# Mixing stage of a one-core transformer kernel reordered: rotation ahead of splits, gating products last, the two channel halves normalised apart, output projection by consecutive channels

## The reference, cut to what matters

```python
h = rmsnorm_2(x, mix_norm[l])
z = h @ w_in[l]                                   # 1024 x 2560: gate u, gate v, q, k, v, 512 columns each
z_sgu = jax.nn.gelu(z[..., :2 * D_SGU], approximate=False)
q = partial_rotary(q, positions)                  # first 16 of 64 channels of each head
k = partial_rotary(k, positions)
y_a = chunked_spatial_gating(z_sgu, sgu_ln_g[l], sgu_ln_b[l], sgu_w_s[l], sgu_b_s[l])
y_b = dilated_mixture_attention(q, k, v).reshape(b, s, D_ATT)
y = jnp.concatenate([rmsnorm_2(y_a, out_norm_a[l]), rmsnorm_2(y_b, out_norm_b[l])], axis=-1)
x = x + y @ w_out[l]
```

## Time and profile before

| what | value |
|---|---|
| median of three runs | 1241.16 us |
| the profiled execution's own time | 1240.6 us |
| its span, first to last instruction | 1238.6 us |
| mean granted PE clock | 0.992 |
| PE busy | 1199.3 us, 97% |
| DVE busy | 777.5 us, 63% |
| ACT busy | 585.3 us, 47% |
| DMA queue q1, share of 16 engines | 51.5% |
| weights read | 203.04 MB |

### The profile page before, as it was taken

How to read it: one execution, slowest core, us unless ns; L and a number is a source line. 1 busy time by engine, 2 the same in 40 slices (tenths; PEclk the granted TensorE clock), 3 DMA queues, 4 the chain that set the end, 5 groups by cost and what they waited for, 6 DMA issues and landing times.

```text
span 1238.6 us, 17664 instructions
## 1 busy us (share of the span) xinstructions
PE 1199.3 (97%) x7063; PEld 1031.1 (83%) x7063; DVE 777.5 (63%) x838; ACT 585.3 (47%) x724; POOL 63.2 (5%) x81
## 2 busy tenths in 40 slices
PE   6889999999999999999999999999979999999997
PEld 5776888888999988888888888888769988888886
DVE  6955766666654556666667666666573645666665
ACT  5445634343656554444345434345554546434443
POOL 2110000000011200000000000000011000000000
PEclk9999999999999999999999999999998999999999
DMA  8254456565544365656565555565432543556561
GB/s 210 80 141 161 156 181 203 173 199 178 172 161 137 120 187 171 197 176 202 178 195 170 189 184 190 182 198 174 139 102 91 182 137 119 183 191 191 182 203 68
DMA packets 157223, 206.04 MB, mean 166 GB/s; under 512 B 8937, under 2 KB 130353, under 8 KB 157169
## 3 DMA queue, kind: packets, MB, share of 16 engines
q1 hardware_dynamic: 156720, 204.51, 51.5%
q10 hardware_dynamic: 448, 0.77, 0.4%
HBM read 203.04 MB, written 1.05 MB: 165 GB/s over the span
## 4 chain that ended last, share of the span: by engine, by line
PE 88%; DVE 5%; ACT 3%; issue 1%; POOL 1%; DMA 1%; ACTq 1%; SPq 0%; POOLq 0%; DVEq 0%
PE outp L745 26%; PE acc L685 19%; PE outp L685 18%; PE outp L747 13%; PE acc L795 2%; PE outp L703 1%; PE outp L715 1%; PE outp L1156 1%; DVE w_lo L2096 1%; DMA raw<-in_even_w_in_dram 1%; ACT w_hi L1569 1%; ACTq L1784 1%; PE acc L1237 1%; ACT arena L1890 1%; PE acc L1379 0%
## 5 line engine op out<-in xcount | busy, mean ns | idle before, releaser
L1569 ACT ACTIVATE w_hi<-raw 128x2048 fp32r<-128x2048 f32 x177 | 339.5, 1918 | 432.4 <-PE outp L747 291.1
L2096 DVE TENSOR_TENSOR w_lo<-raw,w_hi 128x2048 fp32r<-128x2048 f32 x177 | 405.3, 2290 | 199.0 <-ACT w_hi L1569 199.0
L745 PE MATMUL outp<-h_pair,w_hi 128*128 128x512 f32 x1056 | 374.7, 399 | 0.0
L747 PE MATMUL outp<-h_pair,w_lo 128*128 128x256 f32 x1056 | 296.6, 281 | 0.0
L745 PEld LDWEIGHTS outp<-h_pair,w_hi 128*128 128x128 f32 x1056 | 198.5, 188 | 49.5
L747 PEld LDWEIGHTS outp<-h_pair,w_lo 128*128 128x128 f32 x1056 | 199.4, 189 | 1.1
L685 PE MATMUL acc<-w_hi,f_hi 128*128 128x512 f32 x352 | 138.0, 392 | 0.0
L685 PE MATMUL acc<-w_lo,f_hi 128*128 128x512 f32 x352 | 137.6, 391 | 0.0
L685 PE MATMUL acc<-w_hi,f_lo 128*128 128x512 f32 x352 | 137.3, 390 | 0.0
L745 PE MATMUL outp<-m_pair,w_hi 128*128 128x512 f32 x336 | 118.0, 394 | 0.0
L685 PE MATMUL outp<-w_hi,h_pair 128*128 128x512 f32 (+1 forms) x416 | 115.4, 365 | 1.0 <-DVE w_lo L2096 0.8
(11 more groups left out here) (322 smaller groups left out, 1421.8 us busy)
## 6 DMA issues: line engine op xcount, KB each, us to landing
raw<-in_ffn_w_gate_dram SPq DMA_DIRECT2D x44, 1024.0 KB, 5.6
raw<-in_ffn_w_up_dram SPq DMA_DIRECT2D x44, 1024.0 KB, 5.6
raw<-in_ffn_w_down_dram SPq DMA_DIRECT2D x44, 1024.0 KB, 4.9
raw<-in_odd_w_in_dram SPq DMA_DIRECT2D x12, 1024.0 KB, 5.3
raw<-in_w_in_dram SPq DMA_DIRECT2D x10, 1024.0 KB, 5.2
raw<-in_even_w_in_dram SPq DMA_DIRECT2D x5, 1024.0 KB, 9.2
raw<-in_even_w_out_dram SPq DMA_DIRECT2D x4, 1024.0 KB, 6.9
raw<-in_cross_wk_dram SPq DMA_DIRECT2D x4, 1024.0 KB, 5.9
```

Source lines behind the costliest of these rows:

```text
L745: nc.tensor.matmul(bank.rearrange("p (a l) -> p a l", l=L), wh, x[:, :, c, :], start=c == 0, stop=c == C - 1, skip_group_check=True)
L747: ins = nc.tensor.matmul(bank[:, 0:L], wl, x[:, 0, c, :], start=False, stop=c == C - 1, skip_group_check=True)
L1569: A(w_hi[:, slot(u), :], raw[:, u % RAW, :], ACT.Copy).then_inc(w_hi_ready, 1)
L2096: tt(w_lo[:, slot(u), :], raw[:, u % RAW, :], w_hi[:, slot(u), :].bitcast(F32), ALU.subtract).then_inc(w_lo_ready, 1)
```

## The change

1. *Rotation.* On DVE the rotation stands ahead of the split of u0+5.
2. *Scores.* On DVE split u0+7 stands between fronts 1 and 2, fronts 3 and 4 ahead of split u0+9, front 5 behind it, and the second part of the layer norm behind all of them.
3. *Gating products.* On PE they stand behind j=9 instead of behind j=8.
4. *End of the stage on PE.* Transposes b=0, `mem_v1` half 0, transposes b=1, `mem_v1` half 1, transposes of the normalised gating half (8), the value products of both b, `mem_v2`, `mix_out` quarter 0, transposes of the attention half (8), quarters 1 to 3.
5. *Norms.* The gating half of y is squared, scaled and split into hi and lo before the value products, the attention half after them. `norm_bank` gives the two halves places of their own in the `acc` ring.
6. *Layout.* `w_out` is loaded by `by_c` (partition p holds rows p, 128+p, ...), so that its first four chunks belong to the gating half, and the gains are loaded as 4 single values to each of 128 partitions for each half.

No arithmetic is added or left out; the count of matmuls, transposes, splits and DVE and ACT operations stays. The diff, cut:

```diff
-                ("dpt0", 3), ("dpv0", 1), ("dpt1", 3), ("dpv1", 1), ("norm6", 4),
+                ("dpt0", 3), ("dpt1", 3), ("norm6", 2), ("dpv0", 1), ("dpv1", 1), ("norm6b", 2),
...
-        late_loads += [(g_ab[64 * j:64 * j + 64, :], a[n][0].rearrange("(p c) -> p c", c=C))
+        late_loads += [(g_ab[:, 4 * j:4 * j + 4], a[n][0].rearrange("(c p) -> p c", p=P))
...
-                load_out(UNITS["mix_out"], by_p(a["w_out_2"][0]))
+                load_out(UNITS["mix_out"], by_c(a["w_out_2"][0]))
...
PE:
-                    if j == 8:
-                        pe.wait_ge(ln_ready, 1)
...
+                pe.wait_ge(ln_ready, 1)
+                emptied(pe, ACC["ws"], 3)
+                for i in range(2):
+                    k = ACC["sgu"] + i
+                    acc_taken(pe, k)
...
+                def flip_half(h):
+                    pe.wait_ge(xn_v, 2 * NTH[6] + 1 + h)
+                    if h == 1:
+                        pe.wait_ge(xn_a, NTH[6] + 1)
+                    for q in (2 * h, 2 * h + 1):
+                        k = norm_bank(6, q)
+                        acc_taken(pe, k)
+                        for c in range(2):
+                            for t in range(T):
+                                ins = flip(acc[:, k % NB, c * L + t * P:c * L + (t + 1) * P],
+                                           xn[:, t, (2 * q + c) * P:(2 * q + c + 1) * P])
+                        ins.then_inc(acc_ready, 1)
                 for b in range(2):
                     probs_t(ACC[f"dpt{b}"], b, [dsc[:, i, :] for i in range(2)], exp_done,
                             lambda b, j: 3 * b + 2 + j)
+                    mem_half("mem_v1", b)
+                flip_half(0)
+                out_emptied(pe, k0 + 8, 2)
+                for b in range(2):
                     emptied(pe, ACC[f"dpt{b}"], 3)
...
-                norm(6)
-                for half_ in range(2):
                     mem_half("mem_v2", half_)
-                proj_out(UNITS["mix_out"], OUT["mix_out"], chunks(6))
...
+                out_m(0)
+                flip_half(1)
+                for j in range(1, 4):
+                    out_m(j)
...
ACT:
                     for j in range(3):
                         acc_copy(ACC[f"dpt{b}"] + j, dpt[:, b, j * 512:(j + 1) * 512])
-                emptied(act, ACC["sgu"], 2)
+                    if b == 0:
+                        emptied(act, ACC["sgu"], 2)
+                        squares(6, y_nat, [(0, 0), (1, 0)])
+                mem_copy("mem_v1")
+                norm_parts(6, g_ab, qs=(0, 1))
+                split(u0 + 12)
                 for b in range(2):
                     emptied(act, ACC[f"dpv{b}"])
-                squares(6, y_nat)
+                squares(6, y_nat, [(0, 1), (1, 1)])
                 norm_rows(6, y_nat)
-                mem_copy("mem_v1")
-                split(u0 + 12)
-                norm_parts(6, g_ab)
+                mem_copy("mem_v2")
                 split(u0 + 13)
-                mem_copy("mem_v2")
+                norm_parts(6, g_ab, qs=(2, 3))
...
DVE:
-                split(u0 + 5)
                 out_emptied(dve, k0, 4)
...
                 tt(x2, r[2], r[3], ALU.add).then_inc(rot_done, 1)
+                split(u0 + 5)
                 split(u0 + 6)
-                split(u0 + 7)
...
-                for n in range(3):
-                    front(n)
+                front(0)
+                front(1)
+                split(u0 + 7)
+                front(2)
...
                 split(u0 + 8)
+                front(3)
+                front(4)
+                split(u0 + 9)
+                front(5)
                 dve.wait_ge(ln_rms, 1)
...
-                split(u0 + 9)
-                for n in range(3, 6):
-                    front(n)
                 split(u0 + 10)
...
                 split(u0 + 11)
+                for t in range(T):
+                    dve.wait_ge(rms_ready, RMS[6] + t + 1)
+                    ins = ts(xn[:, t, 0:512], y_nat[:, t, 0:512], rms[:, NTH[6], 2 * t:2 * t + 1], None, ALU.mult)
+                ins.then_inc(xn_v, 1)
+                norm_back(6, g_ab, qs=(0, 1))
...
-                norm_front(6, y_nat)
                 split(u0 + 12)
-                norm_back(6, g_ab)
+                dve.wait_ge(rms_ready, RMS[6] + 3)
+                ts(xn[:, 0, 512:], y_nat[:, 0, 512:], rms[:, NTH[6], 1:2], None, ALU.mult).then_inc(xn_v, 1)
                 split(u0 + 13)
+                norm_back(6, g_ab, qs=(2, 3))
```

More of the change, by code:

```diff
@@ L442, in x_whole, with norm_bank @@
                 out_emptied(eng, k, 4)
+        def norm_bank(n, q):
+            return ACC["norm6b"] + q - 2 if n == 6 and q >= 2 else ACC[f"norm{n}"] + q
         def x_piece(h):
@@ L823, in chunks @@
             def chunks(n):
-                return lambda q: emptied(pe, ACC[f"norm{n}"] + q)
+                return lambda q: emptied(pe, norm_bank(n, q))
             def flip_rows(t):
@@ L1332, in mix @@
                         scores(ACC["dsc"] + 3, 1, q_of, k_of)
-                    if j == 8:
-                        pe.wait_ge(ln_ready, 1)
[L1335 to L1344, removed]
+                pe.wait_ge(ln_ready, 1)
[3 more added lines that the diff above has]
+                    acc_taken(pe, k)
+                    for g in range(4):
+                        gg = 4 * i + g
+                        ins = nc.tensor.matmul(acc[:, k % NB, g * P:(g + 1) * P], ws_t[:, gg, :],
+                                               zv[:, :, gg * 64:(gg + 1) * 64], start=True, stop=True)
+                    ins.then_inc(acc_ready, 1)
[10 more added lines that the diff above has]
+                                           xn[:, t, (2 * q + c) * P:(2 * q + c + 1) * P])
+                        ins.then_inc(acc_ready, 1)
                 for b in range(2):
@@ L1360, in mix, with out_m @@
                 for half_ in range(2):
-                    mem_half("mem_v1", half_)
-                norm(6)
-                for half_ in range(2):
                     mem_half("mem_v2", half_)
-                proj_out(UNITS["mix_out"], OUT["mix_out"], chunks(6))
+                def out_m(j):
+                    proj_quarter(UNITS["mix_out"] + j, OUT["mix_out"] + 2 * (j % 2), j // 2,
+                                 chunks(6) if j % 2 == 0 else None, last=j == 3)
+                out_m(0)
+                flip_half(1)
+                for j in range(1, 4):
+                    out_m(j)
             def cross():
@@ L1477, in norm @@
                 pieces = [p for p in x_order(n) if p[0] == 1 or n not in (0, 8)]
+                if n == 6:
+                    for j, (t, h) in enumerate(pieces):
+                        pool.wait_ge(sq_a, SQ_A[n] + j + 1)
+                        r, q = [v[:, i, 2 * t + h:2 * t + h + 1] for v in (rms, ss)]
+                        own.link(gp.tensor_scalar(r, q, 2 / D, EPS, ALU.mult, ALU.add))
+                        gp.tensor_tensor(r, r, half[:, 0:1], ALU.pow).then_inc(rms_ready, 1)
+                    return
                 for t in range(T):
@@ L1483, in norm @@
                             pool.wait_ge(sq_a, SQ_A[n] + pieces.index((t, h)) + 1)
[L1484 to L1492, removed]
+                    r = rms[:, i, 2 * t:2 * t + 1]
+                    own.link(gp.tensor_scalar(r, ss[:, i, 2 * t:2 * t + 1], ss[:, i, 2 * t + 1:2 * t + 2], EPS,
+                                              ALU.add, ALU.add))
+                    gp.tensor_tensor(r, r, half[:, 0:1], ALU.pow).then_inc(rms_ready, 1)
             def root(x, n, scale, eps, done):
@@ L1622, in norm_whole, with norm_parts @@
                     ins.then_inc(acc_free[k % NB], 1)
-            def norm_parts(n, gain, dst=h_hi):
-                for q in range(4):
-                    k = ACC[f"norm{n}"] + q
+            def norm_parts(n, gain, dst=h_hi, qs=range(4)):
+                for q in qs:
+                    k = norm_bank(n, q)
                     written(act, k)
@@ L2128, in norm_front, with norm_back @@
                     return
[L2129 to L2138, removed]
+                dve.wait_ge(rms_ready, RMS[n] + 1)
+                ts(xn[:, 0, :], src[:, 0, :], rms[:, NTH[n], 0:1], None, ALU.mult).then_inc(xn_v, 1)
+                dve.wait_ge(rms_ready, RMS[n] + 2)
                 ts(xn[:, 1, 0:512], src[:, 1, 0:512], rms[:, NTH[n], 2:3], None, ALU.mult).then_inc(xn_v, 1)
-            def norm_back(n, gain, hi=h_hi, lo=h_lo):
-                for q in range(4):
-                    k = ACC[f"norm{n}"] + q
+            def norm_back(n, gain, hi=h_hi, lo=h_lo, qs=range(4)):
+                for q in qs:
+                    k = norm_bank(n, q)
                     dve.wait_ge(h_hi_ready, 8 * NTH[n] - 8 + 2 * q + 2)
```

3 lines of the change are left out of this document (1 added, 2 removed).

## The result

The changed kernel takes 1223.89 us (median of four, 1222.97 to 1224.15) against 1240.24 for the kernel before: a ratio of 0.9867, 95% interval 0.985 to 0.9884, 16.35 us less. The forecast was 1225.5 within 1223.2 to 1230.5, and a gain of 15.7.

A forecast was written before the change was run, and what follows sets the result against it. PE was taken as the bound, busy 97% of the span; 9.9 us of standing plus 6.1 of low clock made 16.0 won, less 0.3, so 1240.6 - 15.7 = 1224.9, median 1225.5, range 1223.2 to 1230.5.

The forecast's parts named there:

- The sign given for this: If right, the stretch from the end of j=4 to `mix_out` takes 60 us, where it took 75.88.
- Standing, 9.9: PE's idle time between the end of j=4 and `mix_out`, 9.94 us, all to be won.
- list of seven waits: PE's idle times: rotation 2.57, split u0+8 0.48, layer norm 1.11, bank 1.84, value copies 1.22, probability copies 1.83 and 0.89.
- Low clock, 6.1: PE at 1.2 GHz for part of four windows behind idle times; 5.3 to 6.8 us, middle 6.1 taken.
- the two ways to price it: Low clock's cost in four windows: by granted clock 6.8 us in sum, by pairs of rows 1.3 to 1.7 each.
- 0.3 given back for margins: Taken off the 16.0 us gain because four margins are 0.5 to 0.9 us and DVE rows have links.
- margins missed: Splits u0+9, u0+14, layer norm or bank late by about 0.7, each with a 1.5 dip; 1229.6 us, chance 0.10.
- clock falls in the transposes: Three groups of transposes on PE lose 1.5 us each to the low clock; 4.5, 1230.0 us, chance 0.04.
- only the rotation counts: ACT's copies stay late, so only 2.57 + 1.4 us is won; 1237.0 us, chance 0.03.
- "slower", the new wait on ACT: ACT's queue waits for the late gating products, holding copies and splits behind it; some 1245 us, chance 0.03.
- The first dip goes with the rotation: Moving the rotation ahead of the split removes PE's 2.57 us wait and the first low-clock stretch; PE 4.0 earlier.
- Layout, 0: New loads of `w_out` and the gains cost 0 to 0.2 us in the second feed-forward stage; 0 taken.

The follow-up runs named there:

- no_cover: Changed kernel with value products right behind the transposes, both `mem_v1` halves after them, bank plan and `norm_back` moved to match; 1227.57 us, ratio 0.9895.
- front_before_split: Changed kernel with front 5 ahead of split u0+9 on DVE; 1222.78 us, ratio 0.9866.
- more_transposes: Changed kernel with each of the 16 transposes of q and k made six times in the same place; 1232.93 us, ratio 0.9938.
- rotation_back: Changed kernel with its first point taken back, split u0+5 ahead of the rotation on DVE; 1227.66 us, ratio 0.9877.
- rotation_only: Kernel before with one edit, the rotation ahead of split u0+5 on DVE; 1237.79 us, ratio 0.9972.
- layout_only: Kernel before with only the layout of `w_out` and the gains changed, and the norm's transposes to match; 1242.47 us, ratio 1.0007.
- norm_before_split: Changed kernel with the layer norm's second part ahead of split u0+9 on DVE, front 5 behind it; 1227.22 us, ratio 0.9897.
- split_last: Changed kernel with split u0+9 behind both front 5 and the layer norm's second part on DVE; 1228.82 us, ratio 0.9889.
- old_score_order: Changed kernel with points 2 and 3 taken back: old order of splits, fronts and layer norm, gating products behind j=8; 1231.1 us, ratio 0.9913.

## Why the prediction was right, point by point

The sum was right in its kind, standing plus low clock, and 1.8 us too small in the stage (15.7 against 17.48). That the forecast of 15.7 lies nearer to the 16.35 of the whole time is in part luck: in the profiled executions 0.94 us of the stage's gain was lost ahead of the stage, which the sum doesn't contain. The sign given for this, 60 us from the end of j=4 to `mix_out`, came out at 57.3 (876.64 to 933.94) with 8 transposes, 0.9 us, fewer in it.

- *Standing, 9.9.* Measured 9.84. The prediction's list of seven waits was complete and each went.
- *Low clock, 6.1.* This term was too small: busy time fell by 7.6. Of the two ways to price it, the granted clock's (6.8) was nearer, and I took the middle with the lower one. The pairs of rows were off since the durations in these rows overlap. Nine transposes that "take 1.19" suggested 2.1 for 16; start to start 16 take 1.67 (876.48 to 878.15). What is above 6.8, 0.8 us, I have not traced to a cause; busy time can grow at the full clock too, as the 0.58 of `no_cover` shows.
- *0.3 given back for margins.* None was missed. The order on DVE came out as laid end to end: the rotation's start was put at 871.4 and lies at 871.5 once the 0.94 later start of the stage is taken off. The tightest margins were where they were named, splits u0+9 and u0+14, each 0.1 or less where 0.5 was worked out. That both held was near; `front_before_split` shows that a miss of 0.28 would have cost 0.1 us.
- *Rival "margins missed".* Its price, 0.7 and a dip of 1.5 for each miss, was wrong: misses of 0.28, 0.83 and 0.65 brought no dip, and one of 0.28 lengthened the stage by 0.08. Two misses of 0.7 would so have cost some 1.4 us (an estimate), not 4.4.
- *Rival "clock falls in the transposes".* Ruled out by `more_transposes`.
- *Rival "only the rotation counts".* `mem_v1` is a real cover, 3.4 us, and the order of scores and gating products is worth more than the rotation.
- *Rival "slower", the new wait on ACT.* ACT begins the squares of the gating half at 916.19, right behind the copies and without an idle time, since DVE is done with the gating at 915.65. It costs nothing, as worked out.
- *"The first dip goes with the rotation".* True in the changed kernel (`rotation_back`: 1.70). In the profiled execution of `rotation_only` the total loss stayed instead. If that isn't chance of one execution, one step of the argument was too simple: a dip doesn't belong to one wait.
- *Halves apart.* The prediction gave this part no price of its own; it is 0.7.
- *Layout, 0.* Measured 0.07 the other way in the stage, no change in time.

Taken back one by one, the parts are worth 4.1 (rotation), 6.8 (scores, layer norm, gating), 3.4 (cover) and 0.7 (halves), 15.0 in sum. The missing 2.5 of 17.5 is in the clock. The four kernels add 11.1 us of standing, more than the 9.84 that was won, but only 3.9 of busy time against 7.64: with one part undone, PE stands less often in all, and fewer of its waits bring a dip (one or none in these kernels, four in the kernel before).

## What to carry to other kernels

Where PE is the bound and still stands, list its waits, find for each what the waiting work really needs, and put independent PE work (here the halves of a projection that nobody waits for) between producer and consumer; then lay the serving engine's queue end to end and compare each end with the time at which PE comes for it. Price the standing by its length, but price the low clock for the stretch as a whole, from the granted clock: here it came with the longer or crowded waits, and what one wait gave back differed between surroundings. The stage's own length in the trace repeated to 0.01 us in the changed kernel, where PE hardly stands, and the kernel before and `layout_only`, with the same waits and four dips each, agree to 0.07. But a stage with waits near the length that brings a dip should be profiled more than once.

## What was new about the hardware

Each of these is from the profiled executions named, one for each kernel.

- A single stand of PE of 2.35 us in dense work left the clock at 2.4 GHz (`norm_before_split`); 2.57 to 2.58 us brought 1.66 to 1.70 us of clock loss (before, `layout_only`, `rotation_back`), 3.95 us brought 3.42 (`split_last`). Stands of 1.25 and 0.99 with 4 us of work between brought none (`no_cover`).
- The same two stands (1.10 to 1.11 and 1.83 to 1.84, 1.2 us of work between) brought 3.4 us at 1.2 GHz in three kernels (before, `layout_only`, `old_score_order`) and 6.8 us in a fourth (`rotation_only`). The losses seen are near 1.7 or 3.4 and nothing between. Which of the two falls due isn't told by the length of the stand alone; this stays open.
- Nor is the moment of the fall. The clock fell 2.1 us into the stand of `rotation_back` and 2.6 us into that of `split_last`; in the kernel before it fell only when PE was at work again, 0.2 us behind the rotation's stand and 2.1 to 2.2 us behind the two stands for the copies.
- 96 transposes in a row keep the clock up, at 0.108 us each.
